# Column tiles inside k-tiles: reordering the matmuls of each weight piece in a two-layer fp32r decoder trunk

## What is computed

```
for i in range(DEPTH):
    h = _rmsnorm(x, attn_norm_g[i])
    mix = _stick_breaking_attention(h, ...) if i % 2 == 0 else _dsa_attention(h, ...)
    x = x + mix
    h = _rmsnorm(x, ffn_norm_g[i])
    x = x + _conv_ffn(h, w_up, conv_w, conv_b, w_down)
```

## Time and profile before

| | us |
|---|---|
| median of 3 runs | 2233.77 |
| the profiled execution, its own time | 2232.74 |
| its span, first to last instruction | 2230.9 |
| TensorE matmuls busy | 2220.7 |
| TensorE weight loads busy | 1956.3 |
| VectorE busy | 1495.7 |
| ScalarE busy | 1165.7 |

### The profile page before, as it was taken

The page is one execution under the profiler, slowest core; times in us unless marked ns, Lnnn a source line. Parts: engine busy times, 40 slices in busy tenths (PEclk is TensorE's granted clock), DMA queues, the critical chain, the costliest instruction groups (busy, mean ns, idle before and its releaser), DMA issues. The chain is left out here.

```text
span 2230.9 us, 35512 instructions
## 1 busy us (share of the span) xinstructions
PE 2220.7 (100%) x12842; PEld 1956.3 (88%) x12842; DVE 1495.7 (67%) x1772; ACT 1165.7 (52%) x1394; POOL 2.5 (0%) x9
## 2 busy tenths in 40 slices
PE   9999999999999999999999999999999999999999
PEld 8888898888888888888889888888888888888888
DVE  7666556677777777555578887677777777774444
ACT  7555555555555555444455456555555555553332
POOL 0000000000000000000000000000000000000000
PEclk9999999999999999999999999999999999999999
DMA  7555545555555556555565544455555555556554
GB/s 268 162 169 175 172 161 180 194 184 191 185 197 179 197 179 199 191 191 191 190 204 199 179 151 131 152 180 189 190 194 187 187 191 191 185 193 203 198 194 136
DMA packets 113543, 412.05 MB, mean 185 GB/s; under 512 B 12736, under 2 KB 13376, under 8 KB 113472
## 3 DMA queue, kind: packets, MB, share of 16 engines
q1 hardware_dynamic: 112464, 407.49, 55.3%
q10 hardware_dynamic: 576, 1.97, 0.2%
q0 software_dynamic: 432, 1.57, 0.2%
HBM read 408.88 MB, written 2.10 MB: 184 GB/s over the span
## 5 line engine op out<-in xcount | busy, mean ns | idle before, releaser
L667 DVE TENSOR_TENSOR w_lo<-raw,w_hi 128x1024 fp32r<-128x1024 f32 x772 | 938.1, 1223 | 679.8 <-ACT w_hi L263 674.2
L1191 PE MATMUL psum<-xg,w_hi 128*128 128x512 f32 (+1 forms) x3936 | 1360.0, 391 | 2.5 <-DVE xg L682 2.5
L263 ACT CAST w_hi<-raw 128x1024 fp32r<-128x1024 f32 x772 | 804.4, 1049 | 781.5 <-PE psum L1191 778.2
L1191 PE MATMUL psum<-xg,w_lo 128*128 128x256 f32 (+1 forms) x3936 | 1093.9, 278 | 0.0
L1191 PEld LDWEIGHTS psum<-xg,w_hi 128*128 128x128 f32 x3936 | 736.8, 187 | 158.4 <-issue 2.2
L1191 PEld LDWEIGHTS psum<-xg,w_lo 128*128 128x128 f32 x3936 | 744.0, 189 | 2.5 <-issue 2.2
L1191 PE MATMUL psum<-hid,w_hi 128*128 128x512 f32 x1408 | 488.2, 391 | 0.0
L1191 PE MATMUL psum<-hid,w_lo 128*128 128x256 f32 x1408 | 394.2, 280 | 0.0
L1191 PEld LDWEIGHTS psum<-hid,w_hi 128*128 128x128 f32 x1408 | 263.3, 187 | 57.7
L1191 PEld LDWEIGHTS psum<-hid,w_lo 128*128 128x128 f32 x1408 | 266.1, 189 | 0.0
L1191 PE MATMUL psum<-att,w_hi 128*128 128x512 f32 x512 | 178.7, 393 | 0.1
(11 more groups left out here) (152 smaller groups left out, 891.8 us busy)
## 6 DMA issues: line engine op xcount, KB each, us to landing
raw<-w_all SPq DMA_DIRECT2D x772, 512.0 KB, 3.4
xres<-x_in SPq DMA_DIRECT2D x4, 512.0 KB, 7.2
cst<-consts_in ACTq DMA_DIRECT2D x2, 768.0 KB, 5.7
out_t<-xres POOLq DMA_DIRECT2D x3, 512.0 KB, 4.1
out_t<-xres SPq DMA_DIRECT2D x4, 128.0 KB, 1.8
vecs<-vecs_in ACTq DMA_DIRECT2D x1, 354.0 KB, 6.4
avg_d<-consts_in SPq DMA_DIRECT2D x1, 64.0 KB, 9.3
vecs<-vecs_in ACTq DMA_DIRECT2D x1, 32.0 KB, 4.2
```

Source lines behind the costliest of these rows:

```text
L263: act.copy(w_hi[:, c % RING, :], raw[:, c % RING, :]).then_inc(hi_ready, 1)
L667: dve.tensor_tensor(w_lo[:, c % RING, :], raw[:, c % RING, :], f32(w_hi[:, c % RING, :]), ALU.subtract).then_inc(lo_ready, 1)
L1191: return pe.matmul(o, lhsT, rhs, start=start, stop=True, skip_group_check=True)
```

## The change

For every piece but the last of the kernel, the loops change places: the k-tile is outside, the column tile inside. The low matmul of a tile no longer follows its own high one; it is issued one place later, after the high matmul of the next tile. With four column tiles the order of tiles and banks in a piece becomes H0 H1 L0 H2 L1 H3 L2 H0 L3 H1 L0 H2 L1 H3 L2 L3. With two column tiles it is H0 H1 L0 H0 L1 H1 L0 H0 L1 ..., so every low matmul is followed by a high one into its own bank. The last piece (`by_col`) keeps its order. In the first piece the waits for activation tiles stand once ahead of each k-tile.

```diff
-                for ct in range(cols // P):
-                    for kk in range(kts):
-                        w = slice(kk * cols + ct * P, kk * cols + (ct + 1) * P)
-                        k = k0_ + kk
-                        if by_tile and ct == 0:
-                            pe.wait_ge(xg_tile, kk + 1)
-                        mm(psum[:, bank0 + ct, :], w_hi[:, s, w], act_in[:, k, :], first and kk == 0)
-                        last = mm(psum[:, bank0 + ct, 0:T], w_lo[:, s, w], act_in[:, k, 0:T])
-                    if by_col:
+                def high(ct, kk):
+                    w = slice(kk * cols + ct * P, kk * cols + (ct + 1) * P)
+                    return mm(psum[:, bank0 + ct, :], w_hi[:, s, w], act_in[:, k0_ + kk, :], first and kk == 0)
+
+                def low(ct, kk):
+                    w = slice(kk * cols + ct * P, kk * cols + (ct + 1) * P)
+                    return mm(psum[:, bank0 + ct, 0:T], w_lo[:, s, w], act_in[:, k0_ + kk, 0:T])
+
+                if by_col:
+                    for ct in range(cols // P):
+                        for kk in range(kts):
+                            high(ct, kk)
+                            last = low(ct, kk)
                         last.then_inc(col_done, 1)
-                if not by_col:
-                    last.then_inc(piece_used, 1)
+                    return
+                behind = None
+                for kk in range(kts):
+                    if by_tile:
+                        pe.wait_ge(xg_tile, kk + 1)
+                    for ct in range(cols // P):
+                        high(ct, kk)
+                        if behind:
+                            low(*behind)
+                        behind = ct, kk
+                low(*behind).then_inc(piece_used, 1)
```

## The result

The changed kernel takes 2260.61 us (median of 4 runs, 2260.38 to 2260.78) against 2233.94 before (2232.78 to 2234.16): ratio 1.0121, 95% interval 1.0109 to 1.0134. It is slower by 26.7 us. The prediction said slower, 2241.8 us within 2230 to 2262.

A forecast was written before the change was run, and what follows sets the result against it. TensorE was taken as never short of work, so time is matmul count times start-to-start step. Banks 0, order of highs and lows 8.0 us, waits 0, added to the median 2233.77, gave 2241.8 us, range 2230 to 2262.

The forecast's parts named there:

- the forecast's own case: Whole kernel slower by +4.5 to +16 us, 2238 to 2250 us, chance 0.40.
- rival B: 591 pieces: slow pace takes over between the borders, all 58 ns each, 34 us, 2268 us; half 2255; chance 0.13.
- Part 1: Steps across PSUM banks: other bank neighbours change nothing, taken as 0, with bounds of nothing and a 13 ns gain.
- rival C: Each step from high to low: the bank was the cost, 13 ns saved, 2160 us; a third 2209; chance 0.10.
- Part 2: Run of highs and lows in 591 pieces with four column tiles: 13.5 ns more each, 8.0 us in sum.
- the entry: First step from H to H in a piece: about 10 ns more than a settled one.
- the two lows: The L L at a piece's end: 3.5 ns more per piece.
- the slow pace between the borders: Alternating pairs between H H and L L of a piece: taken at 0, bound 7 x 6.3 ns.
- Two-column pieces: 104 pieces with two column tiles: lose 1.4 us or gain at most 5.2 us, put at 0.
- Part 3: Signals and waits throughout the kernel: no instruction added or removed, copies and fetches queue as before, 0.
- Rival A: Each piece settles into its own pattern with the settled steps: neutral, 2233.8 us, within 2229 to 2238; chance 0.34.
- Rival D: Cycling through four banks makes the clock fall to 1.2 GHz: 2280 us with a tenth of pieces hit; chance 0.01.

The follow-up runs named there:

- experiment 3: Kernel before with sizes strictly alternating, but in pieces of four column tiles each matmul goes to another bank than the one before it: 2232.51 us, ratio 0.9997.
- experiment 2: Kernel before, column tile still walked first, but each low matmul issued one place behind: 2260.55 us, ratio 1.0119.
- experiment 1: Kernel before with the k-tile walked outside and the column tile inside, each low still right behind its own high: 2233.28 us, ratio 1.0.
- experiment 12: Kernel before with the order of the change only in the 104 pieces with two column tiles: 2235.11 us, ratio 1.0005.
- experiment 7: Kernel before with lows one place behind in one piece, the ninth of layer 0's up projection, after the settling matmuls: 2234.04 us, ratio 1.0001.
- 10: Kernel before with lows one place behind in two pieces, the ninth and thirteenth of layer 0's up projection: 2246.17 us, ratio 1.0059.
- 11: Kernel before with lows one place behind in three pieces, the ninth, thirteenth and sixteenth of layer 0's up projection: 2233.93 us, ratio 0.9999.
- experiment 5: Kernel of experiment 1 with the order of the change in the first piece of each four-column-tile group (60 pieces): 2257.83 us, ratio 1.0109.
- 8: Kernel before with lows one place behind in one piece, the third of layer 0's up projection, ahead of the settling matmuls: 2233.21 us, ratio 0.9999.

## Why the prediction was right, and by how much it was off

The direction was right, and 2260.6 us lies in the stated range, but only 1.4 us below its upper end. It lies outside 2238 to 2250, the range of the forecast's own case, and the loss of 26.7 us is 3.3 times the forecast's 8.0. What holds it inside is the room that the range left for rival B. The direction was earned by the mechanism; that the range held was in part luck.

**Part 1 held.** Steps from high to low across banks cost and give nothing that can be told (experiment 3), so the value taken, 0, was right and rival C is out. The neighbouring rows were a sound proxy.

**Part 2 had the right mechanism and one mis-sized term.** The disturbed neighbours, H H and L L, are the cause: experiment 2 has them without the walk and takes the same time as the change, experiment 1 has the walk without them and takes the time of before. Of the three terms per piece, the entry was priced at 10 ns and measured 12.5; the two lows at 3.5 and measured nothing more. The third, the slow pace between the borders, was taken at 0, "since the pace in the rows holds through stretches longer than a piece". It measured 34.5 ns. That sentence was the failed step: the pace holds until something disturbs it, and the change disturbs it at both borders of every piece. The sum was 13.5 ns for each of 591 pieces; the trace has 46.7, and 591 x 46.7 ns = 27.6 us of the 28.1.

So the outcome lies closest to rival B, which put all three terms at 58 ns and 34 us, and to which I gave 0.13. Its price was high by a seventh pair (between H H and L L a piece has six), by the 4 ns of the lows, and by a pace of 352 and not 353. The argument that spoke against it, 474 us at the fast pace, showed only that an undisturbed stream keeps its pace. The check that the prediction named says the same: the 2736 matmuls behind the settling matmuls of layer 0 took 474.3 us before and 482.3 after, where the forecast had 476.4 and B 484.

**Two-column pieces** were put at 0 between -5.2 and +1.4 us. The attention stages grew by 1.1, and some 0.6 of it is left when their ten pieces with four column tiles are taken off. Layer 0's stretches at 347 lost what experiment 12 shows; those at 353 gained only 1 to 2 ns a pair.

**Part 3 held.** No wait appeared; L682 is still the longest, 2.2 us. Rival A is out by the interval. Rival D is out too: the clock row didn't move. The Trainium skill, "TensorE: Matmul & The Clock Gate", section "A second HAM failure mode: psum-queue depth-cycling", tells of a kernel whose clock fell back when its matmuls cycled through the banks; experiment 3 changes banks at every matmul of most pieces, with the clock at 1.00 and no time lost, so this kernel doesn't show it. D's price was also summed wrongly: by the prediction's own 640 ns for 320, a tenth of the pieces (59 x 8 pairs) would cost 151 us and give about 2385, not 2280. C's had a step too many: the new order has 7 steps from high to low in a piece, not 8. Neither changes the forecast.

**The formula's gap.** The Trainium skill gives columns / 2.4 + 2.5 ns for isolated matmuls ("TensorE: Matmul & The Clock Gate", section "Back-to-back issue gap"). The estimate for a pair worked out from it, 325 ns, is 22 ns below the fastest pace seen in any of the fourteen kernels.

## What to carry to other kernels

When the matrix engine is busy all the time, the busy share says nothing more; count matmuls in a fixed window, or take start to start over a dozen of them, before and after. Here a strict alternation of 512 and 256 columns has a pace of 347 or of 353 ns a pair, and a break in the pattern can switch it for hundreds of microseconds, so an edit that only reorders equal work must be judged by the pace behind it and not by its own few nanoseconds. In this kernel spreading successive matmuls over banks gained nothing, so it is no reason for such a reorder.

## What the runs showed that I had not expected

**The pace is a state that survives.** One changed piece left it fast, two made it slow for 251 pieces, three made it fast again (experiments 7, 10, 11), and in experiment 5 it flipped at each group of the down projection. Removing or shortening a run of six tiny matmuls costs 26 us, where they take 0.7 us a layer. What in the engine keeps this state was not found, and no rule was found that says which break leads to which pace; the runs show that the state is there in the pattern of starts, and that it outlasts hundreds of identical pairs.

**It also differs from run to run.** The output projection of layer 1 has no settling matmuls ahead of it. In 65 us of it, before:

```profile
1425.00:1490.00 65.00, 65.00 (x377) 1.00 0.55 181
```

and in the kernel of experiment 7, which is unlike before only in one piece some 1000 us earlier:

```profile
1425.00:1490.00 65.00, 65.00 (x370) 1.00 0.56 176
```

That is fast in one profiled run and slow in the other. 208 pairs at 6.7 ns are 1.4 us. The seven kernels that take the time of before (before and experiments 1, 3, 7, 8, 11 and 12) have one trace each. In the four that hold 377 matmuls in this window the profiled runs took 2232.4 to 2232.8 us; in the three that hold 369 or 370 they took 2234.0 to 2235.5. The 21 runs of the kernel before in the last series also fall into two groups: 8 from 2232.08 to 2232.92 us and 11 from 2233.60 to 2234.39, with two above. That the two groups of one and the same kernel are these two paces fits all of this, but is argued, since the kernel before has only one trace.
